# A two-block transformer kernel on one core: the first tile of x loaded in two parts, and the order of small steps at its closes changed

## The chip, the cores and the metric

The kernel runs on one core of one Trainium2 chip. A core has five engines that run their own instruction streams and meet through semaphores: TensorE (PE in the profile; its weight loads are PEld), VectorE (DVE), ScalarE (ACT), GpSimd (POOL) and SyncE (SP, which here only issues DMAs). The metric is the device time of one execution in microseconds (us), lower is better. The kernel before takes 2281.43 us, the median of three runs (2281.34 to 2281.47).

## The reference

The input x has 512 tokens of 1024 features in f32. Two blocks of two layers each are applied to it, all in f32. What is computed:

```
# first block: layer 0 gated linear attention (GLA), layer 1 sliding-window attention (SWA)
for i in (0, 1):
    x = x + rms_norm(mixer_i(rms_norm(x, ln_mix_pre[i])), ln_mix_post[i])
    f = square(relu(rms_norm(x, ln_mlp_pre[i]) @ w_up[i])) @ w_down[i]      # 1024 -> 4096 -> 1024
    x = x + rms_norm(f, ln_mlp_post[i])
# second block: layer 0 pooling + state-space mixer ("even"), layer 1 two attentions ("odd")
for l in (0, 1):
    x = layer_norm(alpha * x + mixer_l(x), g_mix[l], b_mix[l])
    x = layer_norm(alpha * x + (silu(x @ w_gate[l]) * (x @ w_up[l])) @ w_down[l], g_ffn[l], b_ffn[l])
return x
# GLA, per chunk n of 64 tokens and head: att = tril(q_dec @ k_inv^T)
#   o = rms_norm(att @ v + q_dec @ S_n, g_norm) * silu(g);  S_(n+1) = S_n * decay + k_end^T @ v
```

## The kernel before, in words

The tokens are four tiles of 128 (t = 0 to 3); x stays in SBUF as X[128, 4, 1024]. To keep f32 accuracy, each matrix product is made of three products in a rounded format: activations are split into a high part AH and a rest AL, weights into WH (rounded by ACT, line 335) and WL (the rest, by POOL, line 347), and PE multiplies AH by WH, AL by WH and AH by WL. The weights stream through six slots (NS = 6): SP issues the load of a chunk of 128 rows once a slot is free, ACT rounds it, POOL takes the rest. The order of every engine's instructions is written out by hand in the program, one function per engine and stage (`act_gla`, `dve_gla`, `pe_gla` and so on); nothing is reordered by a scheduler.

**The start** (`sync`, `act_gla`, `dve_gla`, `pool_gla`, `pe_gla`). SP issues x tile 0, x tile 1, the first four weight chunks, x tiles 2 and 3 and more weights. ACT's own DMA queue carries the identity matrix with the exponents for the reciprocal root (`ident`, a part of CK) and the table of per-feature vectors (`vecs`). Then ACT loads its function table. DVE and ACT take half of each sum of squares of tiles 0 and 1; POOL raises it to the power -1/2 (line 581), for which it needs `ident`; ACT and DVE scale a half of tile 0 each (lines 1650 and 1758), DVE scales tile 1, and PE transposes both (line 1508) into four PSUM banks. Until then PE runs 14 matmuls on zeros (line 1517), then transposes the vectors (line 1500, needs `ident` and `vecs`). The first real product, `gla.q`, starts at line 371.

**The GLA outputs** (`pe_gla`: `scores`, `state`, `outputs`; `dve_gla`: `normed`). For each tile t, `scores(t)` writes the first bank of gB, `gB[0]`; DVE masks it out of the bank into SBUF (line 1840); `outputs(t)` writes heads 0 and 1 into one bank and heads 2 and 3 into another, as `gOUT` says; ACT squares them (line 1722), and DVE scales heads 0 to 3 one after the other out of PSUM (`normed`, line 1864, four instructions). A bank may be written again once its last reader is done: `held[b]` names that reader, and `scores(t + 1)` waits for what `held[gB[0]]` says. The `gla.g0` and `gla.g1` products lie between.

**A close with an RMS norm** (`act_rms_close`, `dve_rms_close`; it ends `gla.out`, `mlp0`, `swa.out` and `mlp1`). The product is finished bank by bank, one token tile a bank. For tile 3, ACT squares the sum (`act_put(..., 3, 1, ...)`: line 609 for `gla.out`, which has no other term to add, line 615 in the others). After the last bank PE transposes tiles 0 and 1 of the next input (line 525), ACT copies the transposed blocks out as AH (`act_feat`, line 543 or 537, one call for each of four banks), DVE as AL, and the next product starts. Between them ACT rounds chunks of weights that the next product will use (`late`), and takes the sums of squares of tiles 2 and 3 (line 572).

**The last close** (`dve_ln_last`, `act_ln_close`, `pool_ln_last`, `sync`). PE ends with four token tiles, the fourth in two halves. Per tile DVE adds the product to X (line 790), takes statistics (793, 797, 799), subtracts the mean and multiplies by the gain (805); POOL raises the variance to -1/2 (924). Then "times rstd plus bias" ends the tile: for tile 0 DVE does all of it in one instruction (`dve_ln_out`, line 811); of tile 1 DVE does the first half (839), while ACT scales the second half (915) and POOL adds its bias (932); tile 2 is ACT's and POOL's; tile 3 is shared. SP stores each piece when it is ready; one piece of tile 3 is stored by ACT (line 3332).

## Time and profile before

| | |
|---|---|
| median of three runs | 2281.43 us |
| the profiled execution | 2281.74 us |
| its span in the trace | 2279.9 us |
| PE busy | 2269.9 us, 100% of the span |
| PEld, POOL, ACT, DVE busy | 83%, 59%, 46%, 45% |
| share of PE in the chain that ended last | 97% |

The profiled execution was 2281.74 us, 1.8 us more than the span between the first and last instruction of the trace, and 0.3 us above the median. The chain that ended last is the work followed back from the last instruction, at each step to what released it. A row of a timeline is a group of equal instructions that follow each other: the start of the first in us from the span's start, the time from there to the end of the last, engine, line and operation, what it writes and reads; in brackets the idle time of the engine before it and what ended that.

### The profile page before, as it was taken

What the parts mean: (1) busy time and instruction counts of PE and PEld (TensorE: products, weight loads), DVE (VectorE), ACT (ScalarE), POOL (GpSimd) and SP (SyncE); (2) the same over time, 40 slices, a digit from 0 to 9 for tenths busy, and PEclk for the clock granted to TensorE, in tenths of its full rate; (3) what the DMA queues carried; (4) which work ended last, traced back from release to release, by engine and by line L of the source; (5) the groups of instructions that cost most, each with busy time, mean ns of one, the idle gap of its engine ahead of it and who ended that gap; (6) DMA issues with size and microseconds to landing.
All of it is one profiled execution on the core that took longest, in us unless ns stands there. A gap on an engine that the chain in (4) does not pass through costs nothing.

```text
span 2279.9 us, 29453 instructions
## 1 busy us (share of the span) xinstructions
PE 2269.9 (100%) x11271; PEld 1887.4 (83%) x11271; DVE 1026.7 (45%) x1378; ACT 1042.4 (46%) x1988; POOL 1351.4 (59%) x1010
## 2 busy tenths in 40 slices
PE   9999999999999999999999999999999999999998
PEld 8888888888878888888887888888898778888887
DVE  3423356535474546635547312434242564142534
ACT  4524545455674454543446233434233662334342
POOL 5633688894535778874354355768454504567774
PEclk9999999999999999999999999999999999999999
...
GB/s 193 89 61 61 148 110 75 107 88 66 103 27 135 99 125 107 65 102 95 82 87 35 90 200 68 101 103 57 101 106 79 79 1 93 203 55 114 83 84 74
DMA packets 157235, 213.74 MB, mean 94 GB/s; under 512 B 33647, under 2 KB 81767, under 8 KB 157095
## 3 DMA queue, kind: packets, MB, share of 16 engines
...
q14 instruction: 51, 0.42, 0.1%
...
## 4 chain that ended last, share of the span: by engine, by line
PE 97%; DVE 1%; ACT 1%; DMA 0%; issue 0%; POOL 0%; DVEq 0%; SPq 0%; ACTq 0%
PE PS L371 25%; PE PS L373 22%; PE PS L1043 8%; PE PS L1039 8%; PE PS L1038 8%; PE PS L1083 6%; PE PS L1078 6%; PE PS L1079 6%; PE PS L2074 1%; PE PS L2052 1%; PE PS L525 1%; PE PS L3001 1%; PE PS L2988 0%; PE PS L2037 0%; PE PS L2593 0%; PE PS L2224 0%
## 5 line engine op out<-in xcount | busy, mean ns | idle before, releaser
L347 POOL TENSOR_TENSOR WL<-WS,WH 128x512 fp32r<-128x512 f32 (+1 forms) x644 | 893.5, 1402 | 636.2 <-ACT WH L335 604.6
L335 ACT ACTIVATE WH<-WS 128x512 fp32r<-128x512 f32 (+2 forms) x606 | 373.9, 624 | 779.4 <-PE PS L373 262.6
L347 POOL TENSOR_TENSOR WL<-h_R,WH 128x512 fp32r<-128x512 f32 x240 | 355.5, 1500 | 92.0 <-ACT WH L332 89.7
L371 PE MATMUL PS<-AH,WH 128*128 128x512 f32 (+1 forms) x1008 | 298.5, 353 | 0.3 <-ACT AH L543 0.3
L1038 PE MATMUL PS<-AH,WH 128*128 128x512 f32 x768 | 298.8, 389 | 0.0
L1039 PE MATMUL PS<-AL,WH 128*128 128x512 f32 x768 | 298.8, 389 | 0.0
L371 PE MATMUL PS<-AL,WH 128*128 128x512 f32 (+1 forms) x1008 | 294.8, 349 | 0.0
L371 PE MATMUL PS<-AH,WL 128*128 128x512 f32 x816 | 288.0, 390 | 0.0
L332 ACT ACTIVATE WH<-h_R 128x512 fp32r<-128x512 f32 x240 | 148.0, 630 | 225.7 <-PE PS L1083 94.2
L373 PE MATMUL PS<-WH,AH 128*128 128x512 f32 (+1 forms) x552 | 214.1, 395 | 0.0
L373 PE MATMUL PS<-WH,AL 128*128 128x512 f32 (+1 forms) x552 | 208.4, 384 | 0.0
L373 PE MATMUL PS<-WL,AH 128*128 128x512 f32 (+1 forms) x552 | 208.1, 385 | 0.0
L1043 PE MATMUL PS<-AH,WL 128*128 128x512 f32 x768 | 205.2, 389 | 0.0
L371 PEld LDWEIGHTS PS<-AH,WH 128*128 128x128 f32 x1008 | 165.5, 189 | 26.1 <-issue 1.8
L371 PEld LDWEIGHTS PS<-AL,WH 128*128 128x128 f32 x1008 | 165.6, 189 | 25.0 <-issue 0.7
L371 PEld LDWEIGHTS PS<-AH,WL 128*128 128x128 f32 x816 | 152.7, 188 | 31.6
L1038 PEld LDWEIGHTS PS<-AH,WH 128*128 128x128 f32 x768 | 144.2, 188 | 30.0
L1043 PEld LDWEIGHTS PS<-AH,WL 128*128 128x128 f32 x768 | 144.2, 188 | 29.9
L1039 PEld LDWEIGHTS PS<-AL,WH 128*128 128x128 f32 x768 | 144.1, 188 | 29.9
L1078 PE MATMUL PS<-WH,h_OH 128*128 128x512 f32 x336 | 130.7, 389 | 0.0
L1079 PE MATMUL PS<-WH,h_OL 128*128 128x512 f32 x336 | 130.7, 389 | 0.0
L373 PEld LDWEIGHTS PS<-WL,AH 128*128 128x128 f32 x552 | 103.6, 188 | 20.6
...
## 6 DMA issues: line engine op xcount, KB each, us to landing
WS<-in_mlp_w_up_dram SPq DMA_DIRECT2D x128, 256.0 KB, 2.9
...
```

What stands on the lines that cost most here:

```text
L332: e.activation(WH[:, s, 0:n], source, ACT.Copy).then_inc(hi.sem, hi.tick(i))
L335: e.activation(WH[:, s, 0:n], WS[:, s, 0:n], ACT.Copy).then_inc(hi.sem, hi.tick(i))
L347: e.tensor_tensor(WL[:, s, 0:n], source, WH[:, s, 0:n].bitcast(F32), ALU.subtract).then_inc(lo.sem, lo.tick(i))
L371: return e.matmul(PS[b][0:mw, cs], weight[:, s, m * mw:(m + 1) * mw], x[:, cs], start=start, stop=stop, skip_group_check=head is not None)
L373: return e.matmul(PS[b][:, 0:n], x[:, m * P:(m + 1) * P], weight[:, s, 0:n], start=start, stop=stop, skip_group_check=head is not None or ...
L525: q = e.transpose(PS[b][:, (2 * c + t) * P:(2 * c + t + 1) * P], src(2 * half + t, 2 * j + c), IDENT)
L1038: e.matmul(o, WH[:, s, c], xh, start=kc == 0, stop=False, skip_group_check=True)
L1039: e.matmul(o, WH[:, s, c], xl, start=False, stop=False, skip_group_check=True)
L1043: q = e.matmul(o, WL[:, s, c], xh, start=False, stop=kc == 7, skip_group_check=True)
L1078: e.matmul(o, xh, WH[:, s, :], start=k == 0 and p in ("p1", "p7", "p2"), stop=False, skip_group_check=True)
L1079: e.matmul(o, xl, WH[:, s, :], start=False, stop=False, skip_group_check=True)
L1083: m = e.matmul(o, D.oh[:, q % 2, k, x], WL[:, s, :], start=False, stop=k == 3, skip_group_check=True)
```

## The change

It has five parts. (1) x tile 0 is loaded in two parts of 64 partitions, the lower issued by SP, the upper by ACT; both readers of tile 0 wait for both. The loads of `ident` and `vecs` move on ACT's queue behind the table load and the first ACTIVATE. (2) `gOUT` is turned round: heads 0 and 1 in `gB[0]`, heads 2 and 3 in `gB[3]`. (3) In `act_rms_close`, one chunk of weights less is rounded ahead of the first copy of transposed blocks (five in place of six, four in place of five for `gla.out`), and what is left is rounded after the fourth. (4) In the last close, tile 0's final operation leaves DVE: ACT scales both halves and POOL adds the bias. (5) SP stores tile 0 when POOL has done both halves.

```diff
--- before.py
+++ after.py
@@ -256,7 +256,7 @@
         raw = [[Sig(ctx.enter_context(nc.semaphore(f"raw_landed{b}{k}"))) for k in range(4)] for b in range(4)]
         landed = [Sig(ctx.enter_context(nc.semaphore(f"weight_landed{i}"))) for i in range(NS)]
         ld = {n: Sig(ctx.enter_context(nc.semaphore("ld_" + n))) for n in (
-            "x0", "x1", "x2", "x3", "ident", "vecs", "const", "rows", "gate_up", "gains0", "gains1", "bands",
+            "x0", "x0b", "x1", "x2", "x3", "ident", "vecs", "const", "rows", "gate_up", "gains0", "gains1", "bands",
             "ln_mix0", "ln_ffn0", "rope", "key_rope", "ln_mix1", "ln_ffn1")}
         stored = Sig(ctx.enter_context(nc.semaphore("stored")))
         sigs = [mm, sc, ve, po, hi, lo, stored, *landed, *ld.values(), *itertools.chain(*raw)]
@@ -687,21 +687,20 @@
                 if t < 2:
                     sumsq(t)
             late = weight_steps(weight_hi, e, w, name + ".1", nk, nk - TAIL)
-            for _ in range(5):
+            for _ in range(4 if other is None else 5):
                 next(late)
             if other is None:
                 act_put(e, w, name, 3, 1, BA[3], other)
                 act_feat(e, w, name, 0, BA, gain, free, [0])
             else:
-                run(late)
                 act_feat(e, w, name, 0, BA, gain, free, [0])
                 act_put(e, w, name, 3, 1, BA[3], other)
             act_feat(e, w, name, 0, BA, gain, free, [1])
             sumsq(2)
-            run(late)
             act_feat(e, w, name, 0, BA, gain, free, [2])
             sumsq(3)
             act_feat(e, w, name, 0, BA, gain, free, [3])
+            run(late)
 
         def dve_rms_close(e, w, name, other, w_row, wtok, gain, normed, free, head=None):
             if head is not None:
@@ -831,9 +830,8 @@
                 dve_ln_put(e, w, name, t, 1, b1[t], 1.0)
                 dve_ln_var(e, w, name, t)
                 dve_ln_centre(e, w, name, t, g, gtok)
-                if t == 0:
-                    dve_ln_out(e, w, name, 0, b_)
-            ve.name("centred", name, 1, 1)
+                for z in range(2):
+                    ve.name("centred", name, t, z)
             w.wait_ge(po, "rstd", name, 1)
             w.wait_ge(ve, "centred", name, 1)
             e.scalar_tensor_tensor(X[:, 1, 0:512], X[:, 1, 0:512], ST[:, 77:78], b_[:, 0:512], ALU.mult, ALU.add).then_inc(
@@ -908,7 +906,7 @@
                 act_feat(e, w, name, 0, b1, None, free, [3])
             else:
                 run(late)
-                for t, z in ((1, 1), (2, 0), (2, 1)):
+                for t, z in ((0, 0), (0, 1), (1, 1), (2, 0), (2, 1)):
                     c = slice(512 * z, 512 * z + 512)
                     w.wait_ge(po, "rstd", name, t)
                     w.wait_ge(ve, "centred", name, t, z)
@@ -931,6 +929,8 @@
                 w.wait_ge(sc, "scaled", name, t, z)
                 e.tensor_tensor(X[:, t, c], X[:, t, c], b_[:, c], ALU.add).then_inc(po.sem, po.tick("x", name, t, z))
             pool_ln_rstd(e, w, name, 0)
+            add(0, 0, slice(0, 512))
+            add(0, 1, slice(512, D))
             pool_ln_rstd(e, w, name, 1)
             add(1, 1, slice(512, D))
             pool_ln_rstd(e, w, name, 2)
@@ -1466,7 +1466,7 @@
         gA, gB = BB, BA
         gC = gB[1:] + gB[:1]
         gD = [gB[1], gB[2], gB[0], gB[3]]
-        gOUT = [gB[3], gB[3], gB[0], gB[0]]
+        gOUT = [gB[0], gB[0], gB[3], gB[3]]
         gE = [TB[:, j // 2, (j % 2) * 512:(j % 2) * 512 + 512] for j in range(4)]
         gw = d["gla_w_in"][0]
         tri_u = TRI.bitcast(U32).rearrange("p (o c) -> p o c", o=1).broadcast_to((P, 4, P))
@@ -1637,12 +1637,15 @@
             pe_feat(e, w, "gla.out", y_tile, lambda t: (ve, "hn", "gla.out", t), 0, BA, held, range(3))
 
         def act_gla(e, w):
+            e.dma_start(X[64:P, 0, :], d["x"][0, 64:P, :]).then_inc(ld["x0b"].sem, ld["x0b"].tick(0, by=16))
+            w.wait_ge(po, "rank0")
+            e.activation(JUNK[:, 0:16], gRK[:, 0:16].bitcast(F32), ACT.Square).then_inc(sc.sem, sc.tick())
             load(e, "ident", (CK[:, 0:C_PW + 16], d["k_const"][:, 0:C_PW + 16]))
             load(e, "vecs", (TB[0:NV, 0, 0:P], d["k_vecs"]))
-            w.wait_ge(po, "rank0")
-            e.activation(JUNK[:, 0:16], gRK[:, 0:16].bitcast(F32), ACT.Square).then_inc(sc.sem, sc.tick())
             for t in range(2):
                 w.wait_ge(ld[f"x{t}"], 0)
+                if t == 0:
+                    w.wait_ge(ld["x0b"], 0)
                 w.wait_ge(sc)
                 e.activation(JUNK[:, 0:512], X[:, t, 512:D], ACT.Square, accum_out=stc(5, t)).then_inc(
                     sc.sem, sc.tick("sq", "n0", t))
@@ -1746,6 +1749,8 @@
         def dve_gla(e, w):
             for t in range(2):
                 w.wait_ge(ld[f"x{t}"], 0)
+                if t == 0:
+                    w.wait_ge(ld["x0b"], 0)
                 e.scalar_tensor_tensor(Y[:, 2 + t, 0:512], X[:, t, 0:512], 1.0, X[:, t, 0:512], ALU.mult, ALU.mult,
                                        accum_out=stc(0, t)).then_inc(ve.sem, ve.tick("half_sq", t))
                 w.wait_ge(ve, "half_sq", t)
@@ -3356,7 +3361,7 @@
         def sync(e, w):
             def x_in(t):
                 e.dma_start(X[:, t, :], d["x"][0, t * P:(t + 1) * P, :]).then_inc(ld[f"x{t}"].sem, ld[f"x{t}"].tick(0, by=16))
-            x_in(0)
+            e.dma_start(X[0:64, 0, :], d["x"][0, 0:64, :]).then_inc(ld["x0"].sem, ld["x0"].tick(0, by=16))
             x_in(1)
             for i in range(4):
                 weight_in(e, w, i)
@@ -3370,7 +3375,8 @@
             load(e, "gate_up", *[(gE[2][32 * j:32 * j + 16, :], d["gla_w_gate_up"][0, :, :]) for j in range(4)])
             for i in range(NS, len(stream)):
                 weight_in(e, w, i)
-            w.wait_ge(ve, "x", "ffn1", 0)
+            w.wait_ge(po, "x", "ffn1", 0, 0)
+            w.wait_ge(po, "x", "ffn1", 0, 1)
             e.dma_start(out[0, 0:P, :], X[:, 0, :]).then_inc(stored.sem, stored.tick(by=16))
             h0, h1 = slice(0, 512), slice(512, D)
             for t, done, z, c in ((1, ve, 0, h0), (1, po, 1, h1), (2, po, 0, h0), (2, po, 1, h1), (3, po, 2, slice(768, D)),
```

ACT at the start, before. Rows are ACT's instructions in program order; CK holds `ident`, TB `vecs`, WH the rounded weights.

```order
1 L298 DMA CK<-in_k_const_dram 128x144
2 L298 DMA TB<-in_k_vecs_dram 120x128
3 L1643 ACT_TABLE_LOAD
4 L1643 ACTIVATE JUNK<-g_RK 128x16
5 L1647 ACTIVATE JUNK,ST<-X 128x512 x2
6 L1650 ACTIVATE Y<-X,ST 128x512
```

And with the change:

```order
1 L1640 DMA X<-in_x_dram 64x1024
2 L1642 ACT_TABLE_LOAD
3 L1642 ACTIVATE JUNK<-g_RK 128x16
4 L298 DMA CK<-in_k_const_dram 128x144
5 L298 DMA TB<-in_k_vecs_dram 120x128
6 L1650 ACTIVATE JUNK,ST<-X 128x512 x2
```

Half of tile 0 stands where `ident` stood, and `ident` and `vecs` stand behind the table load.

ACT at the close of `gla.out`, before: line 609 is the square of tile 3 at row 87, line 543 the copies of transposed blocks (two instructions a bank), 572 the sums of squares.

```order
86 L335 ACTIVATE WH<-WS 128x512 x5
87 L609 ACTIVATE JUNK,ST<-PS 128x512
88 L543 ACTIVATE AH<-PS,VC 128x256 x4
89 L572 ACTIVATE JUNK,ST<-X 128x1024
90 L335 ACTIVATE WH<-WS 128x512
91 L543 ACTIVATE AH<-PS,VC 128x256 x2
92 L572 ACTIVATE JUNK,ST<-X 128x1024
93 L543 ACTIVATE AH<-PS,VC 128x256 x10
```

With the change:

```order
87 L335 ACTIVATE WH<-WS 128x512 x4
88 L609 ACTIVATE JUNK,ST<-PS 128x512
89 L543 ACTIVATE AH<-PS,VC 128x256 x4
90 L572 ACTIVATE JUNK,ST<-X 128x1024
91 L543 ACTIVATE AH<-PS,VC 128x256 x2
92 L572 ACTIVATE JUNK,ST<-X 128x1024
93 L543 ACTIVATE AH<-PS,VC 128x256 x2
94 L335 ACTIVATE WH<-WS 128x512 x2
95 L543 ACTIVATE AH<-PS,VC 128x256 x8
```

One rounding has gone from in front of the square of tile 3, one from among the copies, and both stand behind the fourth bank's copy.

POOL at the end of the program, before: line 924 is the power, 932 the addition of the bias.

```order
224 L924 TENSOR_TENSOR ST<-ST,CK 128x1 x2
225 L932 TENSOR_TENSOR X<-X,GB 128x512
226 L924 TENSOR_TENSOR ST<-ST,CK 128x1
227 L932 TENSOR_TENSOR X<-X,GB 128x512 x2
228 L924 TENSOR_TENSOR ST<-ST,CK 128x1
```

With the change (lines 922 and 930 are the same two):

```order
224 L922 TENSOR_TENSOR ST<-ST,CK 128x1
225 L930 TENSOR_TENSOR X<-X,GB 128x512 x2
226 L922 TENSOR_TENSOR ST<-ST,CK 128x1
227 L930 TENSOR_TENSOR X<-X,GB 128x512
228 L922 TENSOR_TENSOR ST<-ST,CK 128x1
229 L930 TENSOR_TENSOR X<-X,GB 128x512 x2
230 L922 TENSOR_TENSOR ST<-ST,CK 128x1
```

Two additions, tile 0's, stand between the powers of tiles 0 and 1; on DVE the one instruction of line 811 is gone.

## Rows read from the trace of the kernel before

**Rows 1.** Page, the chain that ended last, by engine.
```profile
PE 97%; DVE 1%; ACT 1%; DMA 0%; issue 0%; POOL 0%; DVEq 0%; SPq 0%; ACTq 0%
```
**Rows 2.** Timeline of PE from 0 to 13 us: start, us, operation, [idle before].
```profile
1.31 6.12 PE L1517 MATMUL PS<-g_RK 128*128 128x512 f32 x14 [1.31 <-POOL g_RK L1894]
7.27 0.27 PE L1500 MATMUL PS<-CK,TB 120*128 120x120 f32 x1
7.88 2.28 PE L1508 MATMUL PS<-CK,Y 128*128 128x128 f32 x16 [0.34 <-ACT Y L1650]
10.16 2.26 PE L371 MATMUL PS<-AH,WH 128*128 128x256 f32 x16
```
**Rows 3.** Timeline of ACT, 0 to 13 us; ACTq is its queue issuing.
```profile
0.74 0.42 ACTq L298 DMA_DIRECT2D CK<-in_k_const_dram  x1
1.91 1.28 ACT L1643 ACT_TABLE_LOAD   x1 [1.91 <-issue]
```
**Rows 4.** Timeline of ACT, 33 to 37 us: a rounding, and the DMA behind it.
```profile
34.75 0.63 ACT L335 ACTIVATE WH<-WS 128x512 fp32r<-128x512 f32 x1 [2.09 <-PE PS L371]
34.76 0.36 ACTq L298 DMA_DIRECT2D GB<-in_ln_mix_post_dram  x1
```
**Rows 5.** DMA queues, 3 to 4 us, then 4 to 5 us: packets, MB, share.
```profile
q1 hardware_dynamic: 62, 0.25, 61.8%
q10 hardware_dynamic: 56, 0.03, 22.0%
...
q1 hardware_dynamic: 103, 0.36, 87.4%
q10 hardware_dynamic: 93, 0.04, 14.7%
```
**Rows 6.** Tile X, 0 to 20 us: from issue to landing of x's four loads.
```profile
DMA to landing us min/median/max: 4.4/5.8/6.9
```
**Rows 7.** Timelines of DVE and POOL, 0 to 13 us.
```profile
6.49 0.72 DVE L1749 SCALAR_TENSOR_TENSOR Y<-X 128x512 f32<-128x512 f32 x1 [0.16 <-DMA X<-in_x_dram]
...
6.49 0.56 POOL L581 TENSOR_TENSOR ST<-ST,CK 128x1 f32<-128x1 f32 x1 [4.77 <-DVE ST L1755]
```
**Rows 8.** Timelines of PE and DVE at the scores of tile 1.
```profile
128.82 0.39 PE L373 MATMUL PS<-WL,AH 128*128 128x512 f32 x1
129.37 2.00 PE L1578 MATMUL PS<-g_QX,g_KX 128*128 128x64 f32 x16 [0.16 <-DVE Y L1864]
...
127.65 1.66 DVE L1864 SCALAR_TENSOR_TENSOR Y<-PS,ST,ROWS 128x256 f32<-128x256 f32 x4 [1.13 <-POOL ST L1924]
```
**Rows 9.** Timelines of ACT and PE at the close of gla.out.
```profile
224.14 2.70 ACT L335 ACTIVATE WH<-WS 128x512 fp32r<-128x512 f32 x5
226.75 0.58 ACT L609 ACTIVATE JUNK<-PS 128x512 f32<-128x512 f32 x1
...
226.18 1.47 PE L525 MATMUL PS<-CK,Y 128*128 128x128 f32 x12
227.93 2.15 PE L371 MATMUL PS<-AH,WH 128*128 128x256 f32 x16 [0.27 <-ACT AH L543]
```
**Rows 10.** Timelines of ACT and PE at the close of mlp0.
```profile
563.60 0.82 ACT L543 ACTIVATE AH<-PS,VC 128x256 fp32r<-128x256 f32 x2
...
562.87 1.91 PE L525 MATMUL PS<-CK,Y 128*128 128x128 f32 x16
```
**Rows 11.** Timelines of DVE, PE and POOL at the last close.
```profile
2263.80 1.28 DVE L811 SCALAR_TENSOR_TENSOR X<-X,ST,GB 128x1024 f32<-128x1024 f32 x1
2265.00 0.68 DVE L790 SCALAR_TENSOR_TENSOR X<-X,PS 128x512 f32<-128x512 f32 x1
...
2272.65 0.28 PE L462 MATMUL PS<-WL,h_FH 128*128 128x256 f32 x1
...
2272.51 2.50 POOL L932 TENSOR_TENSOR X<-X,GB 128x512 f32<-128x512 f32 x2 [1.08 <-ACT X L915]
2274.96 0.55 POOL L924 TENSOR_TENSOR ST<-ST,CK 128x1 f32<-128x1 f32 x1
```

## The prediction

> **What bounds the kernel now.** I read the chain that ended last first: PE holds 97% of it [rows 1], so a step counts only where PE waits, ahead of its first matmul or behind its last. Then I read PE's timeline for such places and set the other engines' timelines beside it. The reader is to see three kinds. At the start PE's work on zeros and the transpose of the vectors end at 7.54, and the transposes of x start at 7.88, released by ACT's half of tile 0; the first real product starts at 10.16 [rows 2]. Inside, PE stands still for tenths of a microsecond at the scores of tiles 1 and 3 [rows 8] and at the four RMS closes [rows 9, 10]. At the end DVE, not PE, has the chain: it still ends tile 0 at line 811 while tile 1's bank waits [rows 11]. The terms below, at their upper ends, come to 2.5 us of 2280, or 0.11%, below the 0.2% that a measurement of this kernel can tell from no change.
>
> **The start.** x tile 0, the first that SP issues, landed 4.4 us after its issue, at 5.14, and the slowest of the four took 6.9 [rows 6]; tile 1 was there at 6.49 [rows 7]. While tile 0 travels the two queues take turns packet by packet, 62 against 56 and 103 against 93 in a microsecond, but q10's packets are small, and the DMA engines are idle for a part of the time: from 3 to 4 us the two shares make 84% [rows 5]. With half of tile 0 on q10, both halves (64 packets each) are through at about 4.1 where 128 on one queue took until 4.4, and tile 1 has 64 packets less ahead of it, 0.6 us at 103 a microsecond, less some 0.2 us for q10's larger packets. So tile 0 comes 0.3 to 0.5 us earlier and tile 1 about 0.4. Against it stands `ident`. ACT issued it at 0.74; now the half tile is issued there, its 0.42 us are followed by the table load of 1.28 [rows 3], and the DMA goes out as the ACTIVATE behind that starts, for a DMA behind an ACTIVATE was issued 0.01 us after that one's start [rows 4]: at about 2.5, 1.76 us later. Bounds for its landing: 4.4 us after that issue is 6.9, 6.9 after it is 9.4, both from loads that met the slow first microseconds [rows 6]; from below, nothing forbids 4.5. I take 6.0: its 128 packets follow q10's 64, which are through at about 4.1, at 93 a microsecond they need 1.4 us [rows 5], and 0.5 is left for the landing, less than the 0.7 that tile 0 shows from its last packets at about 4.4 to 5.14. POOL's power ran at 6.49, released by DVE, not by `ident` [rows 7]; with tile 0 0.4 earlier it is due at 6.1, so 6.0 just does not hold it. The vectors follow `ident` by about 0.8 us, at 6.8, and PE asks for them at 7.27. PE's transposes then start at 7.5, which is also the floor that L1500's end sets [rows 2], and the second tile's, which hang on tile 1, move by 0.4 too. Term: 0.4 us saved, bounds 0.6 saved and 2.9 lost (`ident` at 9.4 in place of the power at 6.49).
>
> By the Trainium skill, "ScalarE: Activation LUTs", section What ACT_TABLE_LOAD costs, a load of 1283 ns is followed by a drain of 1380 ns. The load's length agrees with the row's 1.28 us [rows 3]; a drain ahead of the DMAs would put `ident` 1.4 us later, and by it the start would lose about 1 us in place of winning 0.4.
>
> **The banks.** PE's last matmul ahead of the scores of tile 1 starts at 128.82 and gives way 0.23 us later (the start-to-start distance of the same matmuls); the scores start at 129.37, when the fourth `normed` has ended [rows 8]: 0.32 us of standing still. With heads 0 and 1 in `gB[0]` the second of the four (1.66 us together) releases it, 0.8 us earlier, and PE is the later one. The same is seen at tile 3 (164.99 to 165.53, 0.31). `outputs` waits for the mask of the scores anyway, so the bank it now writes first costs nothing; for the transposes of `gla.o` the released order fits (`gB[0]` is asked for third, `gB[3]` fourth). Term: 0.32 + 0.31 = 0.63 saved.
>
> **The closes.** `gla.out`: five roundings of 0.52 us each take ACT from 224.14 to 226.84, the square starts at 226.75, but PE's bank is done at about 226.34, as the transposes follow at 226.18 [rows 9]. With four roundings ACT is free at 226.26 and the square starts at 226.38: 0.37 earlier, then the copies, then L371 at 227.56. PE's floor is 226.18 + 12 x 0.11 = 227.5, so all of it counts. The sums of squares of tiles 2 and 3 come 0.4 us earlier too, and with them the normalised tile 3, for whose first half PE's second round of transposes stands still from 234.29 to 234.44; I take 0.13 for that. Term 0.5. `mlp0`: the copy starts at 563.60 right behind a rounding; its four transposes (562.87 + 3 x 0.11, and 0.27 for the last) are done at 563.47 [rows 10]; 0.1 is to be had, and PE feels it, since its 16 matmuls from 564.53 on take 2.41 us against 2.15 for the same ones at `gla.out` [rows 9]. `swa.out` has the same rows at 717.26 and 718.18: 0.1. `mlp1` shows 0.06. The roundings that moved (a chunk at each close, two at `gla.out`) are hidden: PE uses these chunks behind the head of the next product, 96 matmuls of 0.12 us, 24 of 0.23 and 16 transposes on, some 18 us, and they are done 5 us on. If that cover went, each would cost up to 0.5 us. POOL starts on the rests only when tile 3 is normalised, and takes them in order at 1.3 us each, so it isn't held either. Sum of the closes: 0.5 + 0.1 + 0.1 + 0.06 = 0.76, bounds 0.4 and 0.9.
>
> **The end.** Line 811 takes DVE from 2263.80 to 2265.00, when line 790 takes tile 1 up; though PE had that bank done at about 2264.55 (the banks follow each other by 18 matmuls of 0.227 us). So tile 1 gains 0.43 of the 1.28 us. Tile 2 is the same pattern 4.08 us on: bank done at 2268.63, line 790 at 2268.96, gain 0.3. Then PE is the later one: the last piece started at 2272.99, needs PE's last matmul, 2272.65 + 0.28 = 2272.93, and gains only 0.03 [rows 11]. What POOL does gains more: its two additions for tile 2 (2.50 us from 2272.51) held the power of tile 3 until 2274.96, 0.6 us after the variance; they now start 0.3 earlier, so the power, ACT's piece, POOL's last addition and SP's last two stores come 0.3 earlier. The work that is added, two ACT scalings of 0.72 us and two POOL additions of 1.3 us, starts when tile 0 is centred at 2263.7 and ends at 2267.1, 0.2 us behind the time (2266.92 less 0.43 is 2266.5) at which tile 1's power could run; that power ends at 2267.6, while DVE is centring tile 1 until 2267.8. It is covered by 0.2 us; without it DVE's tile 1 would be late by as much as POOL. Term 0.3, bounds 0.0 (ACT's store, which waits for DVE alone, lands last) and 0.4.
>
> **Sum.** 0.4 + 0.63 + 0.76 + 0.3 = 2.1 us. Against the profiled execution, 2281.74 with a span of 2279.9, this is 2279.6 and a span of 2277.8; the median of the runs lies 0.3 lower, so 2279.3.
>
> **Rivals.**
> (A) The split brings nothing. It would be so if tile 0 waited for the DMA engines and not for a queue. For it: q1 and q10 already take turns, and from 4 us on their shares make 102% [rows 5]. Against it: the idle part before that. Tile 0 then still lands at 5.1, tile 1 wins a little from `ident` being out of its way; the start gives 0 and the time is 2281.4 - 1.7 = 2279.7. The Trainium skill, "DMA: Bandwidth & Descriptors", section Issuing engines are not separate DMA queues, says so: all issuers share the same 16 DMA engines, and issuing from several saves only the issue time. By this rule 2279.7 is the time.
> (B) `ident` is late. The power waits for it, PE's transposes follow 1.4 us behind, and the start turns from 0.4 saved to a loss. With `ident` at 6.9 the loss is 0.4 and the time 2280.1; with it behind SP's whole backlog, as the tiles that needed 6.9 us were, it is at 9.4, the loss is 2.9 and the time 2281.4 - 1.7 + 2.9 = 2282.6, slower than before. The sign turns where the landing passes 6.49 + 1.7 = 8.2. For it: 1.76 us of later issue and only 0.1 us of slack. Against it: the turns that the queues take, 93 packets a microsecond for q10 beside 103 for q1.
> (C) The end gives nothing, since the last store is ACT's or the three last stores share the DMA engines: 2279.6.
>
> **Chances.** Forecast 0.55; A 0.15; C 0.08; B mild (a loss up to 1 us, 2279.9 to 2280.7) 0.15; B full (2282.6) 0.05; something not seen here 0.02. The forecast's own bounds are 2278.9 (all upper ends) to 2279.9. The range 2278.6 to 2280.8 adds at the lower end the 0.3 us by which an execution can lie off the median, takes in A, C and the mild B and leaves out the full one. None of the cases passes 0.2% (4.6 us) either way, so the same 0.97; faster 0.01; slower 0.02 for what I have not seen.
>
> **What would show it.** Tile 0's first DVE instruction at 4.7 to 4.9 and tile 1's at 6.1; POOL's power released by DVE at 6.1 (B: released later, with DVE's sum long done); L371 at 9.7 to 9.8 in place of 10.16. No idle time ahead of the scores. At `gla.out` 0.4 us less between L525 and L371. At the end DVE idle before its second and third line 789, and the power of tile 3 1.7 us behind PE's last matmul in place of 2.0. The forecast is wrong if PE's first product starts after 10.2, or if PE waits anywhere for a rounding or a rest.

## The result, and the profile after

The changed kernel took 2285.78 us (median of 20 executions, 2284.43 to 2286.55) against 2281.39 for the kernel before (20 executions, 2281.30 to 2281.57): a ratio of 1.0018 with a 95% interval of 1.0012 to 1.0024, 4.4 us slower. That is still inside the 0.2% that was called no change. But the forecast was 2279.3 with a range up to 2280.8: where 2.1 us were to be gained, over twice as much was lost. The profiled execution took 2284.94 us, its span 2283.1: 3.2 us more than before. The twenty executions form two groups. Nine lie between 2284.43 and 2285.07 (middle 2284.68), the profiled one among them, with a mean granted clock of 0.999 or 1.000 each; eleven lie between 2285.74 and 2286.55 (middle 2286.20), all with 0.998. The median falls into the second group; against the first alone the change costs 3.3 us. All twenty of the kernel before lie within 0.3 us, so the second group needs a cause too.

Read against the trace of before, the start times of the same matmuls on PE give the account (a difference falls where PE stood still less, and grows where it stood still more):

| place on PE | before, us | after, us | difference | step |
|---|---|---|---|---|
| first product, L371 | 10.16 | 11.26 | +1.11 | +1.11 |
| scores of tile 1 | 129.37 | 130.10 | +0.73 | -0.37 |
| scores of tile 3 | 165.53 | 165.84 | +0.31 | -0.42 |
| head behind gla.out, first L371 | 227.93 | 227.79 | -0.14 | -0.45 |
| the same head, fifth chunk | 232.26 | 233.25 | +0.99 | +1.13 |
| behind mlp0's close | | | +1.91 | +0.92 |
| behind swa.out's close | | | +2.92 | +1.01 |
| PE's last matmul | 2272.65 | 2275.49 | +2.84 | -0.08 |
| end of the span | 2279.9 | 2283.1 | +3.2 | +0.36 |

Only the banks, the front of one close and, by 0.08, `mlp1` gained. One caution on the first row: the trace of before is of an execution 0.35 us above its median, and its start is a late one, with tile 0 taken up at 5.18 and the first product at 10.16. Seven traces further down leave the start as it was; in them DVE takes tile 0 up between 4.45 and 4.72, and the first product starts between 9.58 and 9.78. Against these the changed start lost 1.5 to 1.7 us and not 1.1.

The page of after, its chain by engine and the row of the head's matmuls:

```profile
PE 97%; ACT 1%; DVE 1%; DMA 0%; POOL 0%; issue 0%; DVEq 0%; ACTq 0%; POOLq 0%
...
L371 PE MATMUL PS<-AH,WH 128*128 128x512 f32 (+1 forms) x1008 | 299.0, 353 | 2.8 <-ACT WH L335 2.7
```

PE has the chain as before [rows 1]; the second row is new: 2.7 us of waiting for ACT's rounding of weights, L335, where the prediction had them hidden, and named a wait for one as a sign that it is wrong. Timeline of PE after, at the closes of gla.out and mlp0 (start, us, operation, [idle before <- releaser]):

```profile
227.79 2.14 PE L371 MATMUL PS<-AH,WH 128*128 128x256 f32 x16
...
233.25 1.27 PE L371 MATMUL PS<-AH,WH 128*128 128x256 f32 x8 [0.98 <-ACT WH L335]
...
571.27 0.74 PE L371 MATMUL PS<-AH,WH 128*128 128x256 f32 x4 [0.86 <-ACT WH L335]
```

and of ACT at the same two places:

```profile
224.36 2.18 ACT L335 ACTIVATE WH<-WS 128x512 fp32r<-128x512 f32 x4
...
231.86 0.82 ACT L543 ACTIVATE AH<-PS,VC 128x256 fp32r<-128x256 f32 x2
232.58 1.15 ACT L335 ACTIVATE WH<-WS 128x512 fp32r<-128x512 f32 x2
...
570.60 0.63 ACT L335 ACTIVATE WH<-WS 128x512 fp32r<-128x512 f32 x1
```

The two roundings of gla.out now run from 232.58, behind all copies, and PE takes the first of the two chunks at 233.25. They are the fifth and sixth chunk of the next product, and these belong to its head.

The start after, timelines of PE, ACT and its queue, DVE and POOL (to be read beside [rows 2, 3, 7]):

```profile
0.74 0.59 ACTq L1640 DMA_DIRECT2D X<-in_x_dram  x1
1.37 1.28 ACT L1642 ACT_TABLE_LOAD   x1 [1.37 <-PEq L3429]
1.44 0.75 ACTq L298 DMA_DIRECT2D CK<-in_k_const_dram  x1
2.22 0.69 ACTq L298 DMA_DIRECT2D TB<-in_k_vecs_dram  x1
6.26 0.69 DVE L1754 SCALAR_TENSOR_TENSOR Y<-X 128x512 f32<-128x512 f32 x1 [6.26 <-DMA X<-in_x_dram]
7.57 1.80 POOL L581 TENSOR_TENSOR ST<-ST,CK 128x1 f32<-128x1 f32 x2 [5.85 <-DVE ST L1760]
8.60 0.29 PE L1500 MATMUL PS<-CK,TB 120*128 120x120 f32 x1 [0.99 <-DMA TB<-in_k_vecs_dram]
9.24 1.97 PE L1508 MATMUL PS<-CK,Y 128*128 128x128 f32 x16 [0.35 <-ACT Y L1653]
```

`ident` went out at 1.44, during the table load, and not at 2.5 behind it. Still everything is later: tile 0 of x by 1.1 us (6.26 for 5.18), the vectors so late that PE waits for them. What releases PE's transposes of x at 9.24 is ACT's half of tile 0, behind POOL's power, and of the two powers in POOL's row the first takes 0.87 us where it took 0.56 before: it starts 0.23 us into DVE's square of tile 1. The busy time of each engine in stretches of 1 us, before and then after, with the granted TensorE clock, the share of the DMA engines and GB/s at the end of a row:

```profile
4.00:5.00 1.00, 1.00 (x4) 0.77 (x3) 0.00 (x0) 0.00 (x0) 0.00 (x0) 1.00 1.02 400
5.00:6.00 1.00, 1.00 (x4) 0.81 (x3) 0.79 (x3) 0.72 (x2) 0.00 (x0) 1.00 1.03 398
```
```profile
4.00:5.00 1.00, 1.00 (x4) 0.78 (x3) 0.00 (x0) 0.00 (x0) 0.00 (x0) 1.00 1.03 242
5.00:6.00 1.00, 1.00 (x4) 0.81 (x3) 0.00 (x0) 0.00 (x0) 0.00 (x0) 1.00 0.96 277
```

The DMA engines are as busy as before (1.02 and 1.03) and move 242 GB/s where they moved 400. So the slots are full; each packet takes longer.

The last close after, timelines of DVE and POOL (to be read beside [rows 11]):

```profile
2267.42 0.69 DVE L789 SCALAR_TENSOR_TENSOR X<-X,PS 128x512 f32<-128x512 f32 x1 [0.89 <-PE PS L373]
...
2269.30 1.75 DVE L804 SCALAR_TENSOR_TENSOR X<-X,ST,GB 128x1024 f32<-128x1024 f32 x1
2271.50 0.75 DVE L837 SCALAR_TENSOR_TENSOR X<-X,ST,GB 128x512 f32<-128x512 f32 x1 [0.44 <-POOL ST L922]
```
```profile
2267.43 2.54 POOL L930 TENSOR_TENSOR X<-X,GB 128x512 f32<-128x512 f32 x2 [1.61 <-ACT X L913]
2269.92 1.54 POOL L922 TENSOR_TENSOR ST<-ST,CK 128x1 f32<-128x1 f32 x1
```

DVE is idle before tile 1, as forecast. But POOL is on tile 0's two additions when tile 1's variance is ready; the power comes 0.7 us late and takes 1.54 us instead of 0.55, the centring beside it 1.75 instead of 1.31, and DVE then waits 0.44 for the power.

### The profile page after: what moved, and what is told of

It is laid out like the page before. It is cut to its first block, busy times and chain, and to the rows that moved or that the text cites. A ratio compares the mean times of both kernels' runs of the same rounds, so it can differ in the third digit from the quotient of the medians.

```text
span 2283.1 us, 29455 instructions
## 1 busy us (share of the span) xinstructions
PE 2269.7 (99%) x11271; PEld 1888.2 (83%) x11271; DVE 1024.6 (45%) x1377; ACT 1044.6 (46%) x1990; POOL 1355.1 (59%) x1012
## 4 chain that ended last, share of the span: by engine, by line
PE 97%; ACT 1%; DVE 1%; DMA 0%; POOL 0%; issue 0%; DVEq 0%; ACTq 0%; POOLq 0%
PE PS L371 24%; PE PS L373 23%; PE PS L1038 8%; PE PS L1043 8%; PE PS L1039 8%; PE PS L1078 6%; PE PS L1079 6%; PE PS L1083 6%; PE PS L2079 1%; PE PS L2057 1%; PE PS L525 1%; PE PS L3006 1%; PE PS L2993 0%; PE PS L2042 0%; PE PS L2598 0%; ACT AH L543 0%
## 5 line engine op out<-in xcount | busy, mean ns | idle before, releaser
L335 ACT ACTIVATE WH<-WS 128x512 fp32r<-128x512 f32 (+2 forms) x606 | 374.2, 624 | 777.7 <-PE PS L373 261.7
L371 PE MATMUL PS<-AH,WH 128*128 128x512 f32 (+1 forms) x1008 | 299.0, 353 | 2.8 <-ACT WH L335 2.7
L371 PE MATMUL PS<-AL,WH 128*128 128x512 f32 (+1 forms) x1008 | 294.7, 349 | 0.0
L371 PE MATMUL PS<-AH,WL 128*128 128x512 f32 x816 | 288.0, 390 | 0.0
L371 PEld LDWEIGHTS PS<-AH,WH 128*128 128x128 f32 x1008 | 165.6, 189 | 28.9 <-ACT WH L335 3.3
L371 PEld LDWEIGHTS PS<-AL,WH 128*128 128x128 f32 x1008 | 165.6, 189 | 24.9 <-issue 0.7
L371 PEld LDWEIGHTS PS<-AH,WL 128*128 128x128 f32 x816 | 152.7, 188 | 31.6
```

The costliest lines, as they stand in the source:

```text
L335: e.activation(WH[:, s, 0:n], WS[:, s, 0:n], ACT.Copy).then_inc(hi.sem, hi.tick(i))
L371: return e.matmul(PS[b][0:mw, cs], weight[:, s, m * mw:(m + 1) * mw], x[:, cs], start=start, stop=stop, skip_group_check=head is not None)
```

## The four parts, each alone

Each is the kernel before with one part of the change (the end with the store that belongs to it). The kernel before, on the same chip, took 2281.35 (31 executions; 30 of them 2281.22 to 2281.59, and one 2282.86, the only one with a mean clock of 0.998). No ratio from here on passes 0.3%, even at the end of its interval, and most intervals take in 1; the smaller differences rest on executions that hardly overlap and on the traces.

**Start** (`x0` in two parts, `ident` and `vecs` written behind the ACTIVATE).

```diff
-            e.dma_start(X[:, 0, :], ...)                  (SP)
+            e.dma_start(X[0:64, 0, :], ...)               (SP)
+            e.dma_start(X[64:P, 0, :], ...)               (ACT, first)
-            load "ident", "vecs"; table load, ACTIVATE    (ACT)
+            table load, ACTIVATE; load "ident", "vecs"    (ACT)
```

> The kernel before with part 1 alone (tile 0 in two parts, identity and vectors behind the table load). Theory P (parts add up as the profile of the changed kernel shows them): the first real product starts 1.1 us later, at about 11.3, nothing later gives it back, so 2282.5; and the runs scatter by about 2 us, since all of the changed kernel's scatter (2284.4 to 2286.6) is made here. Rival Q: the start's loss is taken up by slack before the first close and the time stays within 0.3 us of before, 2281.4. Rival R: the scatter comes from another part, and these runs lie within 0.3 us of each other.

Measured: 2283.91 (2282.84 to 2286.06), +2.6. This part alone loses as much as the closes, and it brings the spread: seven executions with a mean clock of 0.999 have their middle at 2283.09, +1.7, and three with 0.998 or less took 2284.08, 2286.02 and 2286.06. The profiled one is that of 2286.02. By stretch:

```profile
7.00:8.00 1.00, 0.00 (x0) 0.00 (x0) 0.86 (x5) 0.89 (x3) 0.00 (x0) 1.00 1.06 387
8.00:9.00 1.00, 0.00 (x0) 0.02 (x1) 0.86 (x4) 0.36 (x2) 0.86 (x1) 0.96 1.06 404
9.00:10.00 1.00, 0.62 (x2) 0.35 (x3) 0.80 (x4) 0.96 (x2) 0.81 (x2) 0.50 1.06 420
```
```profile
9.01 0.43 PE L1500 MATMUL PS<-CK,TB 120*128 120x120 f32 x1 [2.29 <-DMA TB<-in_k_vecs_dram]
```

PE has nothing to do from 6.7 to 9.0, because its matmuls on zeros are through and `vecs` has not landed, and the granted clock then falls from 1.00 to 0.50, the 1.2 GHz level. It is back at 15.7 us. By then PE is 4.1 us behind the kernel before, having been 1.9 behind at L1508. In the trace of the whole change the same 14 matmuls run until 7.6, PE stands for 1.0 us, and the clock stays at 1.00. The 14 do not take the same time everywhere: they start 0.43 us apart at first and 0.23 us apart later, from about 5.5 us on here, and in the whole change's trace not before the last of them. The column of the granted clock has 1.00 in both cases, so it does not show this difference.

**Banks**.

```diff
-        gOUT = [gB[3], gB[3], gB[0], gB[0]]
+        gOUT = [gB[0], gB[0], gB[3], gB[3]]
```

> The kernel before with the banks of the GLA outputs turned round alone. Theory P: the two waits ahead of the scores of tiles 1 and 3 go, 0.37 and 0.42 us by the changed profile, nothing else moves: 2280.7. Rival: the waits come back at the gating products or the gla.out close (a bank freed later there) and the time is 2281.4.

Measured: 2280.49 (2280.38 to 2282.07; without the highest, at 0.998, up to 2280.58), -0.86. The two waits ahead of the scores are gone, and PE is 0.4 us earlier behind each. At tile 1 (beside [rows 8]) the scores now start 0.23 us behind the matmul before, its usual distance:

```profile
128.33 0.39 PE L373 MATMUL PS<-WL,AH 128*128 128x512 f32 x1
128.56 1.89 PE L1578 MATMUL PS<-g_QX,g_KX 128*128 128x64 f32 x16
```

**Closes**, the moved roundings.

```diff
-            for _ in range(5):
+            for _ in range(4 if other is None else 5):
...
-                run(late)
...
             act_feat(e, w, name, 0, BA, gain, free, [3])
+            run(late)
```

> The kernel before with part 3 alone (roundings moved behind the fourth copy at the RMS closes). Theory P: the moved chunks are the fifth and sixth of the next product, which its head already uses; PE wins about 0.45 us before the first product at gla.out and 0.1 at mlp0 and swa.out, and then stands still about 1 us at each of the three until the rounding is done: 2281.4 + 2.6 = 2284.0. Rival (the prediction's step): the chunks are used 18 us later and nothing waits: 2280.7.

Measured: 2283.92 (2283.84 to 2285.67), +2.6. PE's differences: 0.3 gained ahead of gla.out's head and 1.1 lost in it, so 0.8 lost in all; 1.0 lost in mlp0's head, 1.0 in that of swa.out; 0.1 gained at mlp1.

**End**, tile 0's last operation on ACT and POOL.

```diff
-                if t == 0:
-                    dve_ln_out(e, w, name, 0, b_)
...
-                for t, z in ((1, 1), (2, 0), (2, 1)):
+                for t, z in ((0, 0), (0, 1), (1, 1), (2, 0), (2, 1)):
...
+            add(0, 0, slice(0, 512))
+            add(0, 1, slice(512, D))
```

> The kernel before with parts 4 and 5 alone (tile 0's last operation on ACT and POOL). Theory P: POOL's power of tile 1 runs behind the two additions at the same time as DVE's centring of tile 1 and both are slow (1.54 in place of 0.55 us and 1.75 in place of 1.31), DVE then has all its later work 0.3 to 0.4 us later: 2281.8. Rival (the prediction's step): DVE's slack covers it, tile 3's power comes 0.3 earlier: 2281.1. Second rival: the slow pair is an accident of one execution and the time is 2281.1 to 2281.4.

Measured: 2281.67 (2281.60 to 2282.00), +0.3. The slow pair is there again, so it is no accident of one execution:

```profile
2266.03 1.75 DVE L805 SCALAR_TENSOR_TENSOR X<-X,ST,GB 128x1024 f32<-128x1024 f32 x1
2268.21 0.75 DVE L838 SCALAR_TENSOR_TENSOR X<-X,ST,GB 128x512 f32<-128x512 f32 x1 [0.44 <-POOL ST L923]
```
```profile
2264.15 2.54 POOL L931 TENSOR_TENSOR X<-X,GB 128x512 f32<-128x512 f32 x2 [1.61 <-ACT X L914]
2266.65 1.53 POOL L923 TENSOR_TENSOR ST<-ST,CK 128x1 f32<-128x1 f32 x1
```

The four sum to 2.56 - 0.86 + 2.57 + 0.32 = 4.6 us; the whole change cost 4.4. The two agree so closely in part by luck, since the clock fell in eleven of twenty executions there and in three of ten in the start's run. Without those executions it is 1.7 - 0.86 + 2.57 + 0.32 = 3.8 against 3.3. Within half a microsecond the parts add up, and each can be looked at alone.

## Experiments on the start

These four ran on one chip, on which the kernel before took 2282.05 (2281.72 to 2282.49).

**The split alone**, `ident` and `vecs` first on ACT's queue as before:

```diff
             load(e, "ident", (CK[:, 0:C_PW + 16], ...
             load(e, "vecs", (TB[0:NV, 0, 0:P], d["k_vecs"]))
+            e.dma_start(X[64:P, 0, :], d["x"][0, 64:P, :])...
             w.wait_ge(po, "rank0")
```

> Before, with tile 0 of x in two parts of 64 partitions (SP and ACT), but `ident` and `vecs` first on ACT's queue as before, the second part of x behind them. Theory one (what costs is that the second part of x goes ahead of `ident` and `vecs`, on which PE's first transpose waits): `vecs` lands near 8.0 as before, but the second part of tile 0, issued third at about 2.2, lands late, near 6 to 7 us, tile 0's square on DVE starts at 6.0 to 6.8 instead of 5.2, and PE's transpose of tile 0 about 1 us later than in the kernel before: +1 us or so. Theory two (transfers of x of 64 partitions with 4 KB rows on two queues slow each other, whatever their order): packets of x take 0.24 us and more, as in the changed kernel, the DMA engines move under 300 GB/s from 4 to 6 us, and both parts and `vecs` are late: +2 to +3 us, as the start part alone (+2.6).

Measured: 2287.11 (2285.98 to 2288.24), +5.1, more than either theory said. The second part went out at 1.89; ACT's square of tile 0 started only at 8.13 (5.18 before), and PE's clock had fallen to 0.50 by 10 us; all eleven executions have a mean of 0.998. So being third on its queue costs and the shape costs too, and the run does not part them.

**The order alone**, tile 0 whole:

```diff
-            load(e, "ident", ...)
-            load(e, "vecs", ...)
             w.wait_ge(po, "rank0")
             e.activation(JUNK[:, 0:16], ...)
+            load(e, "ident", ...)
+            load(e, "vecs", ...)
```

> Before, with only the issue of `ident` and `vecs` written behind the ACTIVATE with the table load. In the trace of the changed kernel ACT's queue issued them at 1.44 and 2.22 while the table load ran from 1.37, so theory one (the queue's issues do not wait for the table load or the ACTIVATE; only the issue ahead of them on the same queue holds them) expects `ident` issued at 0.74 as before and no difference: 2281.4, within 0.3. Theory two (the place behind the load delays them) expects `ident` issued at about 2.7 to 3.3, `vecs` landing 1 to 2 us later than in before, PE's first transpose 1 to 2 us later: +1 to +2 us.

Measured: 2281.53 (2281.38 to 2281.85), -0.5. Neither theory said this. Its ACT timeline:

```profile
0.73 1.28 ACT L1641 ACT_TABLE_LOAD   x1 [0.73 <-PEq L3423]
1.30 0.39 ACTq L298 DMA_DIRECT2D CK<-in_k_const_dram  x1
1.73 0.68 ACTq L298 DMA_DIRECT2D TB<-in_k_vecs_dram  x1
...
4.25 0.63 ACT L1647 ACTIVATE JUNK<-X 128x512 f32<-128x512 f32 x1 [2.02 <-DMA X<-in_x_dram]
```

and POOL's at the power:

```profile
5.88 1.81 POOL L581 TENSOR_TENSOR ST<-ST,CK 128x1 f32<-128x1 f32 x2 [4.16 <-DMA CK<-in_k_const_dram]
```

The place in the program holds `ident` for 0.56 us (1.30 for 0.74 [rows 3]), but the queue does not wait for the load's end. Tile 0 has no packets of the two small loads beside it. It is 0.9 us earlier than in the trace of before, and 0.2 to 0.5 earlier than in the seven traces with an unchanged start. PE is 0.35 us earlier at 12 us and 0.2 at its end, but that proves little: the trace of the banks alone, whose start is that of before, is 0.47 earlier at L1508 too. And POOL's row shows where an earlier tile is lost. The power has DVE's sum at 5.4 and waits for `ident` until 5.88; by then DVE squares tile 1 (5.65 to 6.34), and the power takes 0.88 us instead of 0.56. ACT's half of tile 0 starts at 6.79, where the seven others have it at 6.58 to 6.77. Whether the 0.5 is the order's or this chip's is taken up below.

**Both parts of 64 partitions from SP**, `ident` and `vecs` as before on ACT's queue:

```diff
+            e.dma_start(X[64:P, 0, :], d["x"][0, 64:P, :])...   (on SP, behind X[0:64])
```

> Before, with tile 0 of x in two parts of 64 partitions, both issued by SP ahead of tile 1; `ident` and `vecs` alone on ACT's queue, written behind the table load as in the change. Theory one (the second queue's order is the cost): `vecs` lands as before, tile 0 lands at about the same time as before, tile 1 some 0.6 us later by one more issue on SP; +0 to +0.6 us. Theory two (the shape of 64 partitions with 4 KB rows uses the DMA engines badly): packets of x take over 0.2 us each and tile 0 lands 0.5 us or more later than before although it has the queue alone; +1 to +2.5 us.

Measured: 2284.05 (2282.50 to 2284.95), +2.0. Here `ident` and `vecs` are early and SP alone fetches x, yet:

```profile
4.00:5.00 1.00, 1.00 (x4) 0.77 (x3) 0.00 (x0) 0.00 (x0) 0.00 (x0) 1.00 1.08 225
5.00:6.00 1.00, 1.00 (x4) 0.81 (x3) 0.17 (x1) 0.20 (x1) 0.00 (x0) 1.00 0.76 250
```

225 GB/s with the DMA engines fully busy: theory two for the shape. The 2.0 us are not the late data alone, for in this trace too PE stands, from 7.3 to 9.8, and its clock is then at 0.50 for 3.4 us, from 10.0 on. In the expectation `ident` and `vecs` are said to be written behind the table load; the kernel has them in front, as before, which takes their order out of the comparison altogether.

**Two halves over all 128 partitions**, 512 columns each, one on SP and one on ACT (this run with those of the next section, beside 2281.40 for the kernel before):

```diff
-            e.dma_start(X[64:P, 0, :], d["x"][0, 64:P, :])...
+            e.dma_start(X[:, 0, 512:D], d["x"][0, 0:P, 512:D])...
-            e.dma_start(X[0:64, 0, :], d["x"][0, 0:64, :])...
+            e.dma_start(X[:, 0, 0:512], d["x"][0, 0:P, 0:512])...
```

> The start part of the change with one difference: tile 0 of x is cut in two halves of 512 columns, each over all 128 partitions (packets of 2 KB), SP issues one and ACT the other. Theory one (the shape of 64 partitions is what makes x slow: 4 KB packets of 0.24 to 0.29 us, where those of tile 1 took 0.159 in the kernel before): packets of 2 KB take 0.08 to 0.12 us, the DMA engines move 350 GB/s or more from 3 to 6 us, tile 0 is there by about 4.5 us, and the time is at or under that of the kernel before: -0.5 to +0.3 us. Theory two (two queues that fetch x together slow each other, or the second queue starts late): packets of x stay at more than twice the time per byte of tile 1, under 300 GB/s, +1.5 to +2.6 us as the start part of the change.

Measured: 2281.81 (2281.68 to 2281.92), +0.4 where the start part lost 2.6.

```profile
3.00:4.00 1.00, 1.00 (x3) 0.76 (x3) 0.00 (x0) 0.00 (x0) 0.00 (x0) 1.00 1.02 395
4.00:5.00 1.00, 1.00 (x4) 0.78 (x3) 0.29 (x1) 0.33 (x1) 0.00 (x0) 1.00 1.04 406
...
4.71 0.69 DVE L1754 SCALAR_TENSOR_TENSOR Y<-X 128x512 f32<-128x512 f32 x1 [4.71 <-DMA X<-in_x_dram]
6.16 1.82 POOL L581 TENSOR_TENSOR ST<-ST,CK 128x1 f32<-128x1 f32 x2 [4.45 <-DMA CK<-in_k_const_dram]
...
7.86 1.97 PE L1508 MATMUL PS<-CK,Y 128*128 128x128 f32 x16 [0.33 <-ACT Y L1653]
```

The same bytes, queues and order, another shape: about 400 GB/s again, and tile 0 at 4.71. It is the shape, not the second queue. The length of a row is no rival, since the whole tile of the kernel before has rows of 4 KB as well and moved at 400 GB/s (the first pair of rows by stretch above). But nothing is gained. The tile at 4.71 is where the prediction wanted it (4.7 to 4.9), yet the seven traces with an unchanged start have it at 4.45 to 4.72: only the one trace of before was late. And the power again waits for `ident`, until 6.16, and takes 0.89 us, so that PE's transposes of x start at 7.86, as in the trace of before. The first product starts 0.28 us ahead of that trace, and PE loses this again at mlp0's close; its last matmul starts 0.01 us from that of before.

The Trainium skill states this in "SBUF — State Buffer": by section Door 1: The DMA port swizzle, partitions 0 to 63 reach 8 of 16 ports, with 196 GB/s measured against 328 for 128 partitions, and by section "Can I just issue two DMAs to hit both halves?" two transfers to the two halves hardly add up. The traces agree in direction, with 197 to 291 GB/s from 3 to 6 us where halves of 64 partitions lead on their queues, against 360 to 406 with the halves by columns; other loads are under way in these stretches too.

**More matmuls on zeros**: the start part with 24 in place of 14, to test the cause of the spread.

```diff
-            for _ in range(14):
+            for _ in range(24):
```

> The start part of the change alone (which came out at 2283.9 median, with runs from 2282.8 to 2286.1), with 24 instead of 14 of the matmuls that PE runs on the rank-0 rows before its first transpose. They end 10 x 0.23 us later, near 9.0 us, so PE is not idle from 6.7 to 9.0. Theory one (the runs near 2286 are those in which the granted clock falls back to half of full speed after the idle stretch ahead of the first transpose): the runs draw together at 2283 to 2283.9, with none near 2286, and the granted clock is full from about 5.5 us on. Theory two (the spread comes from where the transfers of x land): it stays, 2283 to 2286.

Measured: 2283.38 (2282.69 to 2283.80), +1.3. The granted clock stays up:

```profile
9.00:10.00 1.00, 1.00 (x7) 0.78 (x7) 0.18 (x1) 1.00 (x3) 0.60 (x1) 1.00 1.09 436
```
```profile
8.70 0.72 ACT L1653 ACTIVATE Y<-X,ST 128x512 f32<-128x512 f32 x1 [0.60 <-POOL ST L581]
...
9.75 0.27 PE L1500 MATMUL PS<-CK,TB 120*128 120x120 f32 x1
9.85 2.02 PE L1508 MATMUL PS<-CK,Y 128*128 128x128 f32 x16
```

The executions lie within 1.1 us where they spread over 3.2, none is near 2286, and all eleven have a mean clock of 0.999: theory one, the high executions are those in which the clock fell behind PE's idle stretch. The clocks of the single executions say the same of the whole change (1.5 us between its two groups). They do not explain all of the spread: the seven executions of the start part with 0.999 still lie between 2282.84 and 2284.30. That can be a shorter fall, which three digits do not show (the 3.4 us at 0.50 in the trace with both parts from SP go with a mean of 0.999), or x landing at another time; this is open, and the two kernels ran on different chips. What is left here, 1.3 us, is not all lateness of x and `vecs`. ACT has its half of tile 0 done by 9.4, while PE, without a wait, is at its own matmuls until 9.75 and starts on x at 9.85: up to 0.4 us of this trace's loss is the ten matmuls' own.

## Experiments on the closes and the end

**One rounding of gla.out's close moved**, the rest as before:

```diff
-            for _ in range(5):
+            for _ in range(4 if other is None else 5):
                 next(late)
```

> Before, with only one weight rounding of ACT moved, in the one close that has no other stream (gla.out): 4 instead of 5 roundings ahead of the first copies, the last two of the six ahead of the third quarter's copies as before, so that the 5th and 6th chunk of the next product are rounded before its head asks for them at 232 us. Theory one (the loss of the close part is the wait of the next product's head for the 5th and 6th chunk's rounding behind the fourth quarter's copies, and the gain ahead of it is real): PE's first matmul of the head comes 0.3 to 0.5 us earlier than in before and nothing waits at the fifth chunk: -0.3 to -0.5 us, near 2281.0 where before is 2281.4. Theory two (the gain ahead of the head is given back by the copies of the third quarter in any order): 0 +- 0.15.

Measured: 2281.59 (2281.50 to 2283.12), +0.2: theory two. PE gains its 0.34 us ahead of the head, and nothing waits for a rounding, but behind the sixth chunk it stands:

```profile
233.71 0.27 PE L525 MATMUL PS<-CK,Y 128*128 128x128 f32 x1
234.49 1.75 PE L525 MATMUL PS<-CK,Y 128*128 128x128 f32 x14 [0.51 <-DVE Y L588]
```

Tile 3 is normalised from ACT's square, which starts at 231.51 here and at 231.46 before: ACT has the same instructions ahead of it in either order. So the gain ahead of the head is real and 0.5 us are given back at the next thing that ACT feeds.

**All moved roundings in the middle**, behind the third square:

```diff
-                run(late)
                 act_feat(e, w, name, 0, BA, gain, free, [0])
...
             sumsq(2)
             run(late)
```

> Before, with the moved roundings of all four closes placed in the middle instead of behind everything: behind the third square and ahead of the third quarter's copies, where gla.out's 6th stood already. Theory one (in mlp0's and swa.out's closes the whole loss of 1.0 us each is the place behind the fourth quarter's copies, where the next head's sixth chunk waits for it): no loss in these two, and with gla.out's +0.2 the time is 2281.4 to 2281.7. Theory two (ACT has no slack behind its first copies there, so the rounding delays the third quarter's copies or the fourth tile's square by its 0.6 us wherever it stands): +0.5 us at each of the two closes, 2282.4 to 2282.8.

Measured, beside 2281.35: 2282.39 (2282.21 to 2282.68), +1.0: theory two. PE is 0.1 us or less earlier ahead of mlp0's and swa.out's heads and 0.5 later at the fourth tile's transposes of each, 0.2 + 2 x 0.45 in all. At mlp0:

```profile
570.41 0.27 PE L525 MATMUL PS<-CK,Y 128*128 128x128 f32 x1
571.04 1.86 PE L525 MATMUL PS<-CK,Y 128*128 128x128 f32 x15 [0.36 <-DVE Y L588]
```

ACT has no slack there behind its first copies. Behind everything a rounding costs 1.0 us, in the middle 0.5, ahead of the copies nothing. The place it had was the right one.

**Half of tile 0's last operation left on DVE**: 512 columns on DVE, the other 512 on ACT and POOL.

```diff
                 if t == 0:
-                    dve_ln_out(e, w, name, 0, b_)
+                    ...
+                    e.scalar_tensor_tensor(X[:, 0, 0:512], X[:, 0, 0:512], ST[:, 76:77], b_[:, 0:512], ALU.mult, ALU.add)...
...
-                for t, z in ((1, 1), (2, 0), (2, 1)):
+                for t, z in ((0, 1), (1, 1), (2, 0), (2, 1)):
...
             pool_ln_rstd(e, w, name, 0)
+            add(0, 1, slice(512, D))
```

> Before, with tile 0's last operation of DVE halved: DVE does the first 512 columns (0.75 us by the like half on tile 1), ACT scales and GpSimd adds only the second 512. Theory one (the end part lost because GpSimd's two adds of 1.3 us held its power of tile 1 back until DVE's centring of tile 1 was under way, and the two then slowed each other, 1.54 for 0.55 and 1.75 for 1.31 us): with one add GpSimd is free before tile 1's variance, the power takes 0.55 and the centring 1.31 again, DVE starts tile 1's second half 0.2 to 0.3 us earlier than in before, and the end comes 0.2 to 0.3 us earlier. Theory two (DVE's earlier start of tile 1 is worth nothing because the end hangs on the last tile's PE work): 0 +- 0.1, with power and centring at their old durations.

Measured, beside 2281.40: 2281.09 (2281.02 to 2281.22), -0.3: theory one.

```profile
2266.16 1.31 DVE L805 SCALAR_TENSOR_TENSOR X<-X,ST,GB 128x1024 f32<-128x1024 f32 x1
...
2264.29 1.29 POOL L936 TENSOR_TENSOR X<-X,GB 128x512 f32<-128x512 f32 x1 [1.61 <-ACT X L919]
2266.21 0.55 POOL L928 TENSOR_TENSOR ST<-ST,CK 128x1 f32<-128x1 f32 x1 [0.63 <-DVE ST L799]
```

With one addition POOL is idle when the variance comes, and both operations have their old length. POOL's power for tile 3 then starts 1.7 us behind the end of PE's last matmul in place of 2.0, which is the sign that the prediction named, and the 0.3 is what it gave to the end.

## Putting together what gained

> Before, with what the runs left standing: the two banks exchanged in gla's output product (-0.86 alone), `ident` and `vecs` issued behind the table load with tile 0 of x whole (-0.5 alone), the close of gla.out with one rounding moved, and the end with half of tile 0's operation on DVE. Theory one (the four gains lie one after another on the one path and add up): 0.86 + 0.5 + 0.4 + 0.25 = 2.0 us under the kernel before, 2279.4 where before is 2281.4. Theory two (the close's gain and the banks' are the same idle time of PE, and the end gives nothing): 1.4 us under it.

The kernel: banks, order alone, gla.out's moved rounding, half of tile 0 at the end. Measured, beside 2281.40: 2280.63 (2280.45 to 2281.07), -0.8, less than either theory said. The close was in it with the sign that the run beside it then showed to be wrong.

So two more, beside 2281.35. Banks and the half at the end:

> Before, with the two banks exchanged in gla's output product (-0.86 alone) and half of tile 0's last operation left on DVE (-0.31 alone), nothing else. Theory one (the two gains lie on one path, 2,100 us apart, and add): -1.1 to -1.2 us, 2280.2 where before is 2281.4. Theory two (the banks' gain is partly given back at the fourth tile's transposes of gla.out, as the moved rounding's was): -0.6 to -0.8 us.

Measured: 2280.31 (2280.20 to 2280.46), -1.0; 0.86 and 0.31 add up to 1.17.

The same with the order of the start:

> As e15_two, with `ident` and `vecs` also issued behind the table load, tile 0 of x whole. Theory one (the order alone takes the two small transfers out of the way of tile 0 of x and starts the squares of tile 0 0.9 us earlier, of which PE keeps 0.2 to 0.5): 0.2 to 0.5 us under e15_two. Theory two (PE's first transpose waits for `vecs` either way, and the 0.5 of the order alone was that chip's slower start of the kernel before): within 0.1 us of e15_two.

Measured: 2280.42 (2280.22 to 2281.79), -0.9: theory two. The order alone is worth nothing beside this kernel, and the traces of the two show why: tile 0 is taken up at 4.51 instead of 4.72, but the power waits for `ident` until 6.12 and takes 0.86 us, where it ran at 6.04 in 0.56; the first product starts at 9.79 and 9.78. The 0.5 on the other chip, where the kernel before was itself 0.65 us slower than elsewhere, was not found again; why the kernel before was slower on that chip is left open.

The best version is thus the banks and the half at the end, 1.0 us or 0.05% under the kernel before. Its ratio is 0.9995 with an interval of 0.9986 to 1.0004, so a comparison of this kind doesn't tell it from no change. For it speak the executions, whose highest, 2280.46, lies under the lowest of the kernel before, 2281.27, and the waits that are gone from the traces.

## Why the prediction was wrong, step by step

- **Banks: right.** The term was 0.63, measured 0.86 alone; the trace shows 0.37 and 0.42 in the whole change. The wait was read rightly, its worth a little low.
- **Closes, "the roundings that moved are hidden ... some 18 us": wrong, and the largest error.** The prediction had them as chunks behind the head of the next product. They are its fifth and sixth chunk at gla.out and its sixth elsewhere, which the head uses 4.3 to 5 us after its first matmul; PE then waits 0.9 to 1.0 us for ACT at three closes, 2.7 in all. The price it named for lost cover, up to 0.5 us each, was low as well: 1.0 a close. Term 0.76 saved, measured 2.6 lost.
- **Closes, "Term 0.5" at gla.out: wrong even with the roundings in time.** "All of it counts" held for the head's start, 0.3 to 0.45 us; but the tile 3 that was to be 0.4 earlier is not, since ACT does the same work before its square. The run with the one rounding moved gives +0.2. A gain at one wait was booked without asking what the same engine owes next.
- **Start, "both halves are through at about 4.1": wrong.** The step counted packets and let each take as long as those of the whole tile. With 64 partitions they were slower: tile 0 came 1.1 us later than in the trace of before, and 1.5 to 1.8 later than in the seven others. Term 0.4 saved, measured 2.6 lost in the median: 1.1 to 1.7 by late data, and the rest with the clock, which the prediction did not have at all.
- **Start, `ident`: right to be feared, for a wrong reason.** The table load does not hold the queue. `ident` was issued at 1.44 and landed some 5.9 us later, just ahead of DVE's late sum, so it held nothing in the changed kernel. With the tile early it did: in three runs with the new order and a whole tile, and in the halves by columns, the power waited for it until 5.9 to 6.2 and was slow besides.
- **Start, what it was measured from.** The profile of before has tile 0 at 5.18, late for this kernel. The halves of 512 columns have it where the prediction wanted it, and gain nothing.
- **End, "covered by 0.2 us": wrong.** The text had POOL's additions end at 2267.1 and tile 1's power due at 2266.5, 0.6 us apart and not the 0.2 that it names, and no cover of its start; it then counted on a power of 0.55 us beside the centring, and it took 1.54. Term 0.3 saved, measured 0.3 lost; with one addition the 0.3 was there.
- **Rivals.** A said that the split brings nothing; it was a loss. B had the sign of the start, but in the changed kernel DVE's sum released the power, not `ident`, and the time is past even its full form, 2282.6. None had a loss in the closes. The one that ends "slower than before" was built on the part whose costs looked uncertain, and the largest loss came from the part that was booked at nothing.
